# Two hybrid decoder layers on one core: the second block's values projected by token, its 64 sample tokens in narrow products of their own

## The chip, the cores and the metric

The kernel runs on one core of a Trainium2 chip. The metric is the time of one execution on the device, in microseconds, as the median of the runs shown.

## The reference

Two decoder layers over 1024 prompt tokens and 64 sample tokens (8 sequences of 8), width 1024, float32. Layer 0 mixes tokens with an mLSTM, layer 1 with gated linear attention (GLA); each is followed by a SwiGLU feed-forward network, and each part is wrapped in RMS norms. Cut to what the change touches:

```python
def mlstm_mixer(x, w_in, ...):
    proj = jnp.einsum('bsd,de->bse', x, w_in)
    q, k, v, o, ig, fg = jnp.split(proj, ...)      # 512, 512, 1024, 1024 columns, gates
    ...
    num = jnp.einsum('bhls,bshv->bhlv', A, vc) + ...     # values with tokens as rows
    C_new = ... + jnp.einsum('bshd,bshv->bhdv', kw, vc)
    y = jax.nn.sigmoid(o) * head_rms_norm(h, g_head)

def gla_mixer(x, w_in, ...):
    q, k, v, r, glr = jnp.split(proj, ...)
    o_intra = jnp.einsum('bhls,bshv->bhlv', A, vc)
    y = jax.nn.silu(r) * head_rms_norm(o, g_head)
```

So both mixers take a projected value matrix `v` of 1024 columns, and both multiply it with the token as the contracted index.

## The kernel before, in words

**Tokens and blocks.** The tokens lie in two blocks: block 0 holds 512 prompt tokens, block 1 holds the other 512 prompt tokens and the 64 sample tokens (576). Activations are kept with features on the 128 partitions and tokens in columns: `HH[b]` and `HL[b]`, a high and a low part of each number, of type fp32r. Weights come from HBM in tiles of 128 x 1024 (`w_stage`, three slots), and are split into `w_hi` (ScalarE, line 1444) and `w_lo` (VectorE, line 1796). A dense product is three matmuls for each of eight slices k of the contracted width: `w_lo` with HH, `w_hi` with HH, `w_hi` with HL.

**Units.** `Plan` writes the whole program out as a list of units of one weight tile each: P (mixer projections; 25 for each layer and block: unit 0 the gates, 1 to 8 q and k, 9 to 16 the values, 17 to 24 the output gate), W (output projection), G, U and D (feed-forward). A unit of block 0 is 24 matmuls of 512 columns; one of block 1 is 24 pairs of 288 columns into two PSUM banks (`GW`, line 1002). The small steps of the mixers and norms are tags on units: an engine runs its part of a tag behind its part of the unit. Every engine walks the same list in order. Banks 0 to 3 of PSUM are for units, banks 4 to 7 (`M0` = 4) for the mixers.

**Values of block 0** are projected token-major (`turned`, line 1007). The stationary operand is the activation of 128 tokens, and 512 columns of weights stream past it. Four units (`u.part` 0 to 3, each with two slices k) fill four banks, one for each chunk of 128 tokens; at part 3 the banks are evicted (line 1469 or 1818), and stored by token in `value_scratch` (`VD`). A mixer step loads its chunk from there (`values`, line 801) straight into its operand `V`.

**Values of block 1** are projected like all else, with features on partitions, and stored in `proj_scratch` (`PT`). For each chunk c of 4 to 8 (8 is the samples) the mixer loads them as `vt` (lines 798 and 866), turns them on TensorE with eight transposes (`v_turns`, line 1230) and copies them from PSUM to `V` on ScalarE (`v_copy`, line 1642). The semaphores `v_turned` and `v_copied` count these through `TURNS`.

**Where it stands.** Layer 0: block 1's units P 0 to 14, then the eight W of block 0, then P 15 to 24, then feed-forward units of block 0, on which the mixer steps of block 1 hang: `mload` loads at the first of them, `ma` (scores), `mb` (output), `md` (state), `me` (gating) follow. Block 0's own mixer steps hang on P units 22 to 24 of block 0 and 0 to 13 of block 1. Layer 1: P 0 to 24 of block 1, with `lload` on unit 21, then feed-forward units with `la`, `l1`, `l2`, `lb`, `le`. SyncE issues all loads and stores in the same order of units; evictions go through three slots of `evicted` (`E`), which a store must have left (semaphore `stored`) before they are written again.

```python
for m, (w, x) in enumerate(((wlo, hi), (whi, hi), (whi, lo))):
    for t in range(NG[blk]):
        mm = pe.matmul(ps[:, grp.bank + t, 0:W], wsl(w, k), x[:, k, t * W:(t + 1) * W], ...)
```

Of the kernel before, what the change touches and what calls it, by code (L numbers as in the profile page):

```python
# [13 lines left out]
P = 128  # L14
D = 1024
KD = D // P
# [31 lines left out]
NPROJ = 25  # L48
NW = 3
# [6 lines left out]
class Unit:  # L56
# [3 lines left out]
    def __init__(self, kind, layer, blk, i, j=0):  # L60
# [9 lines left out]
        self.part = (i - 9) % 4 if kind == "P" and blk == 0 and 9 <= i < 17 else None  # L70
# [24 lines left out]
class Plan:  # L95
# [50 lines left out]
    def banks(self):  # L146
# [3 lines left out]
        for u in self.units:  # L150
            by = "dve" if u.kind in "UD" or u.late else "act"
            if u.part is not None:
                if u.part == 0:
                    mine = [Group(0, (at + c) % 4, {held[(at + c) % 4][0]: held[(at + c) % 4][1]}, 0) for c in range(4)]
                if u.part < 3:
                    u.groups.append(Group(n, None, {}, 0))
                    n += 1
                for c, grp in enumerate(mine if u.part == 3 else ()):
                    counts[by] += 1
                    grp.n, grp.ev = n, counts[by]  # L160
                    held[grp.bank] = (by, grp.ev)
# [28 lines left out]
def schedule(plan):  # L190
# [62 lines left out]
    u = mlstm(plan, 0, [(u, u + 1, u + 3, u + 4) for u in range(at["P", 0, 0, 22, 0], at["P", 0, 1, 13, 0], 4)])  # L253
# [34 lines left out]
    u = gla(plan, 1, at["P", 1, 1, 21, 0], [at["G", 1, 0, i, 0] for i in (6, 8, 10, 12, 14)])  # L288
# [40 lines left out]
def mlstm(plan, blk, slots):  # L329
# [18 lines left out]
def gla(plan, blk, first, slots):  # L348
# [3 lines left out]
    for c, u in zip(CHUNKS[blk], slots):  # L352
# [6 lines left out]
        tag(u, "la", c)  # L359
        tag(u + 1, "l1" if c < NC else "l2", c)  # L360
# [80 lines left out]
def memory(nc, ctx):  # L441
# [96 lines left out]
    g.VD = nc.dram_tensor("value_scratch", [2, 4, P, H * DV], F32, kind="Internal").ap()  # L538
# [27 lines left out]
def program(nc, g, plan, a):  # L566
# [42 lines left out]
    def TURNS(layer, c):  # L609

        return 5 * layer + c - 3
# [34 lines left out]
    for u in units:  # L646
# [4 lines left out]
        if u.part is not None:  # L651
            u.places = []
            for c in range(4 if u.part == 3 else 0):
# [53 lines left out]
    with nc.Block() as block:  # L707
        @block.sync
        def _(sp):
# [43 lines left out]
            def evicted(u):  # L753
                if u.kind != "P" or u.i == 0:
                    return
                if u.part is not None:
                    for c, (slot, _) in enumerate(u.places):
                        sp.wait_ge(s["left_dve" if u.late else "left_act"], u.groups[c].ev)
                        sp.dma_start(g.VD[u.layer, c, :, (u.i - 12) * P:(u.i - 8) * P], g.E[:, slot, 0:NT[0]]
                                     ).then_inc(s["stored"][slot], 16)  # L760
# [27 lines left out]
            def m_qkv(c):  # L788
# [6 lines left out]
                if c < 4:  # L795
                    return
                wait(sp, s["v_turned"], TURNS(0, c) - 1)
# [3 lines left out]
            def values(layer, c):  # L801
# [3 lines left out]
                             ).then_inc(s["values_landed"], 16)  # L805

# [54 lines left out]
            def l_v(c):  # L861
                if c < 4:
                    values(1, c)
                    return
# [4 lines left out]
            def lload(c):  # L869
                blk = BLOCK(c)  # L870
                region_free(1, blk)
                landed(1, blk, 16)
                sp.wait_ge(s["b_stored"], 64 * (blk + 1))
                l_qkb(c)
                l_v(c)

            def l_o(c):
                if c in (0, 4):
                    landed(1, BLOCK(c), 24)
                if c >= 4:  # L880
                    sp.wait_ge(s["v_turned"], TURNS(1, c))
# [23 lines left out]
            def me(c):  # L905
                if c < 3:
# [24 lines left out]
            def ss(layer, j):  # L931
                if j == 0 and layer:
                    sp.wait_ge(s["level_done"], 8 * NC + 4)
                elif j == 0:
                    sp.wait_ge(s["s_ready"], NC + 1)
                    sp.wait_ge(s["k_turned"], NC + 1)
                    sp.wait_ge(s["v_turned"], TURNS(0, NC))
# [1530 lines left out]
```

## Time and profile before

| | |
|---|---|
| median of 3 runs | 2584.54 us (2583.43 to 2585.45) |
| profiled execution | 2585.84 us, span 2584.1 us |
| TensorE (PE) | 2567.6 us busy, 99% of the span, 17163 instructions |
| VectorE (DVE) | 1499.2 us, 58% |
| ScalarE (ACT) | 1011.8 us, 39% |
| DMA, hardware queue | 327.79 MB, 40.7% of 16 engines' span |
| chain that ended last | PE 93%, DVE 5%, ACT 2%, issue 1% |

A row of matmuls gives the sum or the mean of their durations, and one matmul's duration covers its way through a pipeline in which the next has begun. What one costs in a stream is therefore read from starts, not from durations: from the start of one row of the timeline to that of a later one, divided by the matmuls between. One matmul of float32 operands leaves two records, one of fp32r operands and one transpose leave one. PEld is the load of the stationary operand that belongs to each matmul.

### The profile page before, as it was taken

To read this page: it belongs to the slowest core of one execution; us is meant where nothing else is said; L and a number is where in the kernel's file an instruction comes from. 1 tells how busy PE (TensorE), PEld (TensorE's weight loads), DVE (VectorE), ACT (ScalarE), POOL (GpSimd) and SP (SyncE) were. 2 spreads that over 40 slices of the span, in tenths; PEclk is the share of its full clock that TensorE was granted. 3 is DMA by queue.
4 is the path that set the end of the run, shared out by engine and by line. 5 is a ranking of instruction groups with operands and counts; after the bars stand their busy time and mean duration, and the time that the engine had idled before them with its cause. 6 is when DMAs were issued, how large, how long until landed. Compare 5 with 4: busy or idle time off the path is not lost.

```text
span 2584.1 us, 40632 instructions
## 1 busy us (share of the span) xinstructions
PE 2567.6 (99%) x17163; PEld 2322.6 (90%) x17163; DVE 1499.2 (58%) x2314; ACT 1011.8 (39%) x1452; POOL 0.2 (0%) x4
## 2 busy tenths in 40 slices
PE   9999999999999999999999999999999999999998
PEld 7899898887988998889999988998887989999998
DVE  6744575556466673357754776338776486434435
ACT  5343355452334342445424444335552343222222
POOL 0000000000000000000000000000000000000000
PEclk9999999999999999999999999999999999999999
DMA  6454545444433333553333343444346334322222
GB/s 222 136 176 155 142 154 161 139 119 154 149 118 106 127 103 98 170 160 95 111 104 105 95 154 110 141 151 125 111 133 189 119 111 141 103 83 83 87 83 91
DMA packets 176704, 330.38 MB, mean 128 GB/s; under 512 B 19964, under 2 KB 93436, under 8 KB 176524
## 3 DMA queue, kind: packets, MB, share of 16 engines
q1 hardware_dynamic: 176524, 327.79, 40.7%
q8 instruction: 136, 2.23, 0.4%
q14 instruction: 44, 0.36, 0.0%
HBM read 271.46 MB, written 56.28 MB: 127 GB/s over the span
## 4 chain that ended last, share of the span: by engine, by line
PE 93%; DVE 5%; ACT 2%; issue 1%; DMA 0%; SPq 0%; DVEq 0%; ACTq 0%
PE ps L1002 81%; PE ps L1016 3%; PE ps L1321 1%; PE ps L1029 1%; PE ps L1409 1%; PE ps L1400 1%; PE ps L1263 1%; DVE Y L1867 1%; PE ps L1251 1%; PE ps L1245 1%; PE ps L1127 1%; DVE w_lo L1796 0%; PE ps L1244 0%; PE ps L1354 0%; PE ps L1355 0%
## 5 line engine op out<-in xcount | busy, mean ns | idle before, releaser
L1002 PE MATMUL ps<-HH,w_lo 128*128 128x288 f32 (+1 forms) x3480 | 944.4, 328 | 0.2 <-DVE w_lo L1796 0.2
L1002 PE MATMUL ps<-HL,w_hi 128*128 128x288 f32 (+1 forms) x3480 | 933.7, 325 | 0.0
L1002 PE MATMUL ps<-HH,w_hi 128*128 128x288 f32 (+1 forms) x3480 | 933.4, 325 | 0.0
L1002 PEld LDWEIGHTS ps<-HH,w_lo 128*128 128x128 f32 x3480 | 589.9, 188 | 49.7 <-issue 5.8
L1796 DVE TENSOR_TENSOR w_lo<-w_stage,w_hi 128x1024 fp32r<-128x1024 f32 x392 | 478.6, 1221 | 258.2 <-ACT w_hi L1444 257.0
L1002 PEld LDWEIGHTS ps<-HL,w_hi 128*128 128x128 f32 x3480 | 589.0, 188 | 42.8
L1002 PEld LDWEIGHTS ps<-HH,w_hi 128*128 128x128 f32 x3480 | 589.1, 188 | 40.8
L1444 ACT ACTIVATE w_hi<-w_stage 128x1024 fp32r<-128x1024 f32 x392 | 412.1, 1052 | 342.5 <-PE ps L1002 307.8
L1867 DVE TENSOR_TENSOR Y<-ps,Y 128x512 f32<-128x512 f32 (+1 forms) x319 | 226.5, 720 | 148.7 <-PE ps L1002 147.8
L1002 PE MATMUL ps<-hid_hi,w_lo 128*128 128x288 f32 (+1 forms) x1052 | 291.4, 331 | 3.1 <-DVE Y L1867 2.5
L1002 PE MATMUL ps<-hid_hi,w_hi 128*128 128x288 f32 (+1 forms) x1052 | 286.9, 327 | 0.0
L1002 PE MATMUL ps<-hid_lo,w_hi 128*128 128x288 f32 (+1 forms) x1052 | 286.8, 327 | 0.0
L1515 ACT ACTIVATE hid_hi<-evicted 128x512 fp32r<-128x512 f32 (+1 forms) x88 | 57.9, 658 | 363.8 <-DVE evicted L1849 363.8
L1002 PEld LDWEIGHTS ps<-hid_hi,w_lo 128*128 128x128 f32 x1052 | 178.4, 188 | 23.1 <-DVE Y L1867 5.9
L1002 PEld LDWEIGHTS ps<-hid_lo,w_hi 128*128 128x128 f32 x1052 | 178.8, 188 | 13.9
L1002 PEld LDWEIGHTS ps<-hid_hi,w_hi 128*128 128x128 f32 x1052 | 178.8, 188 | 13.1
L1849 DVE TENSOR_TENSOR evicted<-ps,evicted 128x512 f32<-128x512 f32 (+1 forms) x88 | 63.5, 722 | 145.5 <-PE ps L1002 145.4
L1807 DVE TENSOR_TENSOR n_sum<-n_sum,n_sq 128x512 f32<-128x512 f32 (+1 forms) x110 | 79.4, 722 | 93.0 <-ACT n_sq L1450 89.1
L1511 ACT ACTIVATE evicted<-ps 128x512 f32<-128x512 f32 (+1 forms) x88 | 54.8, 623 | 176.8 <-PE ps L1002 176.4
L1484 ACT ACTIVATE evicted<-ps 128x576 f32<-128x576 f32 (+1 forms) x64 | 40.8, 637 | 211.3 <-PE ps L1002 211.1
L1852 DVE TENSOR_TENSOR hid_lo<-evicted,hid_hi 128x512 fp32r<-128x512 f32 (+1 forms) x88 | 63.8, 725 | 63.8 <-ACT hid_hi L1515 63.8
L1450 ACT ACTIVATE n_sq<-n_xs 128x512 f32<-128x512 f32 (+1 forms) x64 | 41.6, 657 | 91.2 <-DVE n_xs L1909 84.4
(260 smaller groups left out, 1891.3 us busy)
## 6 DMA issues: line engine op xcount, KB each, us to landing
w_stage<-w_gate_in SPq DMA_DIRECT2D x88, 512.0 KB, 3.6
w_stage<-w_up_in SPq DMA_DIRECT2D x88, 512.0 KB, 3.7
w_stage<-w_down_in SPq DMA_DIRECT2D x88, 512.0 KB, 3.6
w_stage<-w_in_in SPq DMA_DIRECT2D x80, 512.0 KB, 3.8
w_stage<-w_out_in SPq DMA_DIRECT2D x32, 512.0 KB, 3.8
proj_scratch<-evicted SPq DMA_DIRECT2D x48, 288.0 KB, 2.2
proj_scratch<-evicted SPq DMA_DIRECT2D x32, 256.0 KB, 2.1
w_stage<-w_v_in SPq DMA_DIRECT2D x16, 512.0 KB, 4.1
```

What stands on the lines that cost most here:

```text
L1002: mm = pe.matmul(ps[:, grp.bank + t, 0:W], wsl(w, k), x[:, k, t * W:(t + 1) * W], start=(k == first and m == 0), stop=(k == last and m == 2))
L1016: mm = pe.matmul(ps[:, grp.bank, :], x[:, k, t], w[:, n % NW, cols], start=(k == 0 and m == 0), stop=(k == KD - 1 and m == 2))
L1444: act.activation(g.whi[:, n % NW, :], g.wst[:, n % NW, :], ACT.Copy).then_inc(s["w_hi"], 1)
L1450: act.activation(grouped(dst, b) if src.shape != dst.shape else dst, src, ACT.Square).then_inc(s["squared"], 1)
L1484: act.activation(grouped(g.E[:, u.slot, 0:NT[b]], b), bank(grp.bank, b), func, scale=scale).then_inc(s["left_act"], 1)
L1511: act.activation(grouped(g.E[:, c, 0:NT[b]], b), bank(grp.bank, b), ACT.Silu).then_inc(s["left_act"], 1)
L1515: act.activation(g.hh[:, u.i % 2, 0:NT[b]], g.E[:, 2, 0:NT[b]], ACT.Copy).then_inc(s["hid_hi_ready"], 1)
L1796: dve.tensor_tensor(g.wlo[:, n % NW, :], g.wst[:, n % NW, :], g.whi[:, n % NW, :].bitcast(F32), ALU.subtract).then_inc(s["w_lo"], 1)
L1807: dve.tensor_tensor(acc, acc, sq, ALU.add).then_inc(s["summed"], 1)
L1849: dve.tensor_tensor(grouped(pr, b), bank(grp.bank, b), grouped(g.E[:, u.i % 2, 0:NT[b]], b), ALU.mult).then_inc(s["left_dve"], 1)
L1852: dve.tensor_tensor(g.hl[:, u.i % 2, 0:NT[b]], pr, g.hh[:, u.i % 2, 0:NT[b]].bitcast(F32), ALU.subtract).then_inc(s["hid_lo_ready"], 1)
L1867: dve.tensor_tensor(Y, bank(grp.bank, b), Y, ALU.add).then_inc(s["left_dve"], 1)
```

## The change

Three things change, in both layers:

- The projections of block 1 are made in another order (`PROJ`): units 0 to 8, then 17 to 24 (output gate), then 9 to 16 (values). Positions of all tags stay where they were by number, so that with the first 15 positions of layer 0 now stand output gates where values stood.
- The values of block 1's 512 prompt tokens are projected as those of block 0 are: token-major, four units into four banks, 5 evictions at part 3, and stored in `value_scratch`, which now has room for all eight chunks. Chunks 4 to 7 are loaded from there, and their transposes and copies are gone. Only the samples (chunk 8) keep `vt`, eight transposes and a copy.
- The values of the 64 sample tokens are projected in `sample_values`, called as a fifth chunk of each value unit: for each of four output tiles of 128 features, two slices k and three matmuls, of 64 columns each, into bank 6, which is one of the mixers'. Before the first of them PE waits for the mixer steps that used the bank, and the first mixer step behind them (`ma(4)`, `la(4)`) waits for its eviction.

The functions `mload` and `lload` no longer wait for the values; a new step `vload` does, on the unit of `ma(4)` or `la(4)`.

```diff
+PROJ = (tuple(range(NPROJ)), tuple(range(9)) + tuple(range(17, 25)) + tuple(range(9, 17)))
+SAMPLE_BANK = 6
...
-        self.part = (i - 9) % 4 if kind == "P" and blk == 0 and 9 <= i < 17 else None
+        self.part = (i - 9) % 4 if kind == "P" and 9 <= i < 17 else None
...
-        for i in range(i0, i1):
+        for i in PROJ[blk][i0:i1]:
             self.put(Unit("P", layer, blk, i))
...
                     mine = [Group(0, (at + c) % 4, {held[(at + c) % 4][0]: held[(at + c) % 4][1]}, 0) for c in range(4)]
+                    if u.blk:
+                        mine.append(Group(0, SAMPLE_BANK, {}, 0))
...
-        if blk:
-            tag(a + blk, "mv", c)
+        if c == 4:
+            tag(a, "vload", c)
...
-    def TURNS(layer, c):
-
-        return 5 * layer + c - 3
+    def TURNS(layer):
+
+        return layer + 1
...
+                        if c < 4:
+                            sp.dma_start(g.VD[u.layer, 4 * u.blk + c, :, (u.i - 12) * P:(u.i - 8) * P], g.E[:, slot, 0:NT[0]]
+                                         ).then_inc(s["stored"][slot], 16)
+                        else:
+                            sp.dma_start(g.PT[u.i - 4:u.i, :, span(NC)].rearrange("q p t -> p q t"),
+                                         g.E[:, slot, 0:4 * TS].rearrange("p (q t) -> p q t", q=4)
+                                         ).then_inc(s["stored"][slot], 16)
...
+            def vload(c):
+                layer = 0 if vloads.pop() else 1
+                landed(layer, 1, 16)
+                values(layer, c)
...
-                landed(0, blk, 16)
+                landed(0, blk, 8 if blk else 16)
...
+            def sample_values(n, u, grp):
+
+
+                HH, HL = g.HH[1], g.HL[1]
+                if u.part == 0 and u.layer == 0:
+                    pe.wait_ge(s["nat_copied"], 2)
+                    pe.wait_ge(s["gate_act"], 10)
+                    pe.wait_ge(s["state_added"], 4)
+                elif u.part == 0:
+                    pe.wait_ge(s["z_abs"], 8)
+                if u.part == 0 and u.i > 9:
+                    pe.wait_ge(s["left_act"], unit("P", u.layer, 1, 12).groups[4].ev)
+                for q in range(4):
+                    for j in range(2):
+                        k, cols = 2 * u.part + j, slice(j * 512 + q * P, j * 512 + (q + 1) * P)
+                        for m, (x, w) in enumerate(((HH, g.wlo), (HH, g.whi), (HL, g.whi))):
+                            mm = pe.matmul(ps[:, grp.bank, q * TS:(q + 1) * TS], w[:, n % NW, cols], x[:, k, 512:576],
+                                           start=(q == 0 and k == 0 and m == 0),
+                                           stop=(q == 3 and k == KD - 1 and m == 2))
+                return mm
...
             def turned(n, u):
 
+                HH, HL = g.HH[u.blk], g.HL[u.blk]
                 for c, grp in enumerate(u.chunks):
                     if u.part == 0:
                         free(grp)
+                    if c == 4:
+                        mm = sample_values(n, u, grp)
                     t = slice(c * L, (c + 1) * L)
-                    for j in range(2):
+                    for j in range(2 if c < 4 else 0):
...
             def ma(c):
                 n = SIZE(c)
+                if c == 4:
+                    pe.wait_ge(s["left_act"], unit("P", 0, 1, 16).groups[4].ev)
...
-                if c >= 4:
+                if c == NC:
                     v_turns(c, 1, g.x.VT)
```

**TensorE, a value unit of block 1.** Before, each of the 16 such units (8 in each layer) is 24 of these rows (`HH`, `HL` the activations, `w_lo`, `w_hi` the weights, `ps` PSUM):

```order
L1002 MATMUL ps<-HH,w_lo 128x288 x2
L1002 MATMUL ps<-HH,w_hi 128x288 x2
L1002 MATMUL ps<-HL,w_hi 128x288 x2
L1002 MATMUL ps<-HH,w_lo 128x288 x2
L1002 MATMUL ps<-HH,w_hi 128x288 x2
L1002 MATMUL ps<-HL,w_hi 128x288 x2
```

Now the unit ends its fourth chunk of prompt tokens, and the samples' products follow it:

```order
L1060 MATMUL ps<-w_lo,HH 128x512
L1060 MATMUL ps<-w_hi,HH 128x512
L1060 MATMUL ps<-w_hi,HL 128x512
L1043 MATMUL ps<-HH,w_lo 128x64
L1043 MATMUL ps<-HH,w_hi 128x64
L1043 MATMUL ps<-HL,w_hi 128x64
L1043 MATMUL ps<-HH,w_lo 128x64
L1043 MATMUL ps<-HH,w_hi 128x64
L1043 MATMUL ps<-HL,w_hi 128x64
```

In place of 24 pairs of 288 columns a unit has 24 matmuls of 512 columns and 24 of 64; in all units there are 384 of the narrow ones.

**TensorE, the step `la` of layer 1 for a chunk of prompt tokens** (`l_vt` the loaded values, `l_k_decayed` the keys, both turned with the identity `ident`). Before:

```order
L1002 MATMUL ps<-HH,w_lo 128x512
L1002 MATMUL ps<-HH,w_hi 128x512
L1002 MATMUL ps<-HL,w_hi 128x512
L1230 MATMUL ps<-ident,l_vt 128x128 x8
L1303 MATMUL ps<-ident,l_k_decayed 128x128 x4
```

Such eight transposes stand at eight places before (four chunks in each layer), and at none now; those of the samples stay at two.

**ScalarE, the steps of block 0's chunk 3 in layer 0**, beside block 1's projections (`evicted` the evictions, `m_scores` the decays of `ma`, `m_y_normed` the squares of `mb`). Before:

```order
L1484 ACTIVATE evicted<-ps 128x576
L1669 ACTIVATE HH<-m_y_gated 128x8x128
L1625 ACTIVATE m_scores<-m_scores,per_token 128x128 x4
L1630 ACTIVATE m_k_weighted<-ps,per_token 128x128 x4
L1444 ACTIVATE w_hi<-w_stage 128x1024
L1484 ACTIVATE evicted<-ps 128x576
L1651 ACTIVATE m_y_normed,small<-ps,small 128x256 x4
```

Now:

```order
L1533 ACT_TABLE_LOAD
L1533 ACTIVATE evicted<-ps 128x576
L1718 ACTIVATE HH<-m_y_gated 128x8x128
L1481 ACT_TABLE_LOAD
L1674 ACTIVATE m_scores<-m_scores,per_token 128x128 x4
L1679 ACTIVATE m_k_weighted<-ps,per_token 128x128 x4
L1492 ACTIVATE w_hi<-w_stage 128x1024
L1533 ACT_TABLE_LOAD
L1533 ACTIVATE evicted<-ps 128x576
L1481 ACT_TABLE_LOAD
L1700 ACTIVATE m_y_normed,small<-ps,small 128x256 x4
```

Four loads of function tables have come in, since the evictions there are now sigmoids of the output gate. In the whole program ScalarE has 112 of them where it had 105.

## Rows read from the trace of the kernel before

**Rows 1.** The page: busy time, granted clock and the chain that ended last.

```profile
PE 2567.6 (99%) x17163; PEld 2322.6 (90%) x17163; DVE 1499.2 (58%) x2314; ACT 1011.8 (39%) x1452; POOL 0.2 (0%) x4
...
PEclk9999999999999999999999999999999999999999
...
PE 93%; DVE 5%; ACT 2%; issue 1%; DMA 0%; SPq 0%; DVEq 0%; ACTq 0%
```

**Rows 2.** Waits of PE, longest in total.

```profile
PE ps L1029 <- DVE HL L2343: 2.8, 2, 2.2
PE ps L1002 <- DVE Y L1867: 2.5, 6, 0.7
```

**Rows 3.** PE timeline (start, duration), block 1's units: 42 pairs lie between.

```profile
341.18 0.43 PE L1002 MATMUL ps<-HH,w_hi 128*128 128x288 f32 x2
...
352.38 0.43 PE L1002 MATMUL ps<-HH,w_hi 128*128 128x288 f32 x2
```

**Rows 4.** PE timeline, block 0's value units in layer 0: first and last of 192.

```profile
61.03 0.40 PE L1016 MATMUL ps<-w_lo,HH 128*128 128x512 f32 x1
...
104.72 0.39 PE L1016 MATMUL ps<-w_hi,HL 128*128 128x512 f32 x1
```

**Rows 5.** PE timeline at the transposes of chunk 4, layer 0.

```profile
398.68 0.39 PE L1002 MATMUL ps<-HH,w_hi 128*128 128x512 f32 x1
398.90 0.39 PE L1002 MATMUL ps<-HL,w_hi 128*128 128x512 f32 x1
399.13 1.04 PE L1230 MATMUL ps<-ident,m_vt 128*128 128x128 f32 x8
399.92 0.48 PE L1002 MATMUL ps<-HH,w_lo 128*128 128x512 f32 x1
400.24 0.39 PE L1002 MATMUL ps<-HH,w_hi 128*128 128x512 f32 x1
```

**Rows 6.** Line L1384: durations in ns min/median/max, first and last start in us.

```profile
L1384 PEld LDWEIGHTS ps<-batch_rows,m_k_weighted x8: 183/188/188, 648.4 to 649.2; 64*128 64x128 f32 x8
L1384 PE MATMUL ps<-batch_rows,m_k_weighted x8: 252/252/273, 648.4 to 649.2; 64*128 64x8 f32 x8
```

**Rows 7.** Timeline of PE and PEld at narrow matmuls of one column and of 128.

```profile
43.07 0.96 PEld L1186 LDWEIGHTS ps<-ones,Y 1*128 1x128 f32 x8 [0.35 <-issue]
...
138.91 1.05 PE L1215 MATMUL ps<-m_qk 128*128 128x128 f32 x8
...
139.80 0.60 PE L1219 MATMUL ps<-ident,m_qk 128*128 128x128 f32 x4
```

**Rows 8.** Weight loads by shape: count, busy us, mean ns.

```profile
L1002 PEld LDWEIGHTS ps<-HL,w_hi 128*128 128x128 f32 x3480 | 589.0, 188 | 42.8
...
L1263 PEld LDWEIGHTS ps<-ident,m_y_normed 128*128 128x128 f32 x64 | 7.5, 140 | 0.5
```

**Rows 9.** ScalarE timeline at block 0's chunk 3, layer 0.

```profile
231.48 0.65 ACT L1484 ACTIVATE evicted<-ps 128x576 f32<-128x576 f32 x1 [6.53 <-PE ps L1002]
233.61 1.06 ACT L1669 ACTIVATE HH<-m_y_gated 128x1024 fp32r<-128x1024 f32 x1 [1.48 <-DVE m_y_gated L2109]
236.63 1.28 ACT L1625 ACTIVATE m_scores<-m_scores,per_token 128x128 f32<-128x128 f32 x4 [1.96 <-DVE m_scores L2051]
...
240.08 0.65 ACT L1484 ACTIVATE evicted<-ps 128x576 f32<-128x576 f32 x1 [0.21 <-PE ps L1002]
244.35 0.47 ACT L1651 ACTIVATE m_y_normed<-ps,small 128x256 f32<-128x256 f32 x1 [3.62 <-DVE small L2068]
```

**Rows 10.** Line L1484: durations in ns of its table loads.

```profile
L1484 ACT ACT_TABLE_LOAD  x8: 1283/1283/1283, 332.8 to 1746.1; - x8
```

**Rows 11.** Line L1469, block 0's value evictions in layer 1, and their idle time.

```profile
L1469 ACT ACTIVATE evicted<-ps x8: 598/598/599, 1062.6 to 1088.4; 128x512 f32<-128x512 f32 x8
...
DMA value_scratch<-evicted: 2.6, 1
```

**Rows 12.** DMA issues: count, KB each, median us to landing.

```profile
value_scratch<-evicted SPq DMA_DIRECT2D x16, 256.0 KB, 2.3
...
m_v_one<-value_scratch SPq DMA_DIRECT2D x4, 512.0 KB, 4.5
```

**Rows 13.** Windows of 2 us: busy us of PE, PEld, DVE, ACT, POOL, then granted clock.

```profile
1760.00:1762.00 2.00, 2.00 (x86) 1.76 (x85) 2.00 (x7) 0.66 (x1) 0.00 (x0) 1.00 0.09 35
...
1766.00:1768.00 2.00, 2.00 (x133) 1.57 (x131) 1.90 (x4) 1.06 (x1) 0.00 (x0) 1.00 0.59 119
```

More of the change, by code:

```diff
@@ L160, in banks @@
                     grp.n, grp.ev = n, counts[by]
-                    held[grp.bank] = (by, grp.ev)
+                    if c < 4:
+                        held[grp.bank] = (by, grp.ev)
                     u.groups.append(grp)
@@ L252, in schedule @@
         tag(at["P", 0, 0, 12, 0] + 2 * j, t, 0, j)
-    u = mlstm(plan, 0, [(u, u + 1, u + 3, u + 4) for u in range(at["P", 0, 0, 22, 0], at["P", 0, 1, 13, 0], 4)])
+    u = mlstm(plan, 0, [(u, u + 1, u + 3, u + 4) for u in range(at["P", 0, 0, 22, 0], at["P", 0, 1, 0, 0] + 13, 4)])
     assert u <= at["W", 0, 0, 0, 0], (u, at["W", 0, 0, 0, 0])
@@ L359, in gla @@
         tag(u, "la", c)
+        if c == 4:
+            tag(u, "vload", c)
         tag(u + 1, "l1" if c < NC else "l2", c)
@@ L652, in program @@
             u.places = []
-            for c in range(4 if u.part == 3 else 0):
+            for c in range(4 + u.blk if u.part == 3 else 0):
                 u.places.append((turn % 3, stores[turn % 3]))
@@ L861, in l_v @@
             def l_v(c):
-                if c < 4:
+                if c < NC:
                     values(1, c)
@@ L905, in me @@
             def me(c):
-                if c < 3:
+                if c < NC - 1 and c != 3:
                     values(0, c + 1)
@@ L954, in sh @@
                     sp.dma_start(a["n_out"], g.NS[:, :]).then_inc(s["outs"], 16)
-            steps = {"xpart": xpart, "xload": xload, "xstore": xstore, "mload": mload, "mb": mb, "md": md, "lg": lgate, "lload": lload,
+            steps = {"vload": vload, "xpart": xpart, "xload": xload, "xstore": xstore, "mload": mload, "mb": mb, "md": md, "lg": lgate, "lload": lload,
                      "lvt": l_v, "l1": l_o, "lb": lb, "me": me, "la": la, "le": le, "l2": l2, "ss": ss, "sh": sh, "mg3": rows, "last": last}
@@ L1226, in v_turns @@
                 n = SIZE(c)
-                pe.wait_ge(s["vt_landed"], 16 * TURNS(layer, c))
+                pe.wait_ge(s["vt_landed"], 16 * TURNS(layer))
                 wait(pe, s["y_gated"], 9 * layer + c)
@@ L1294, in la @@
                 n = SIZE(c)
+                if c == 4:
+                    pe.wait_ge(s["left_act"], unit("P", 1, 1, 16).groups[4].ev)
                 if c in (0, 4):
@@ L1468, in evict @@
                             wait(act, s["hid_lo_ready"], u.hid0)
-                            act.activation(g.E[:, slot, 0:NT[0]], ps[:, grp.bank, :], ACT.Copy).then_inc(s["left_act"], 1)
+                            cols = slice(0, 4 * TS if grp.bank == SAMPLE_BANK else NT[0])
+                            act.activation(g.E[:, slot, cols], ps[:, grp.bank, cols], ACT.Copy).then_inc(s["left_act"], 1)
                         return
@@ L1637, in v_copy @@
                 n = SIZE(c)
-                if c < 4:
+                if c < NC:
                     return
-                act.wait_ge(s["v_turned"], TURNS(layer, c))
+                act.wait_ge(s["v_turned"], TURNS(layer))
                 wait(act, s["kv"], NC * layer + c)
@@ L1666, in y_high @@
                 if c in (0, 4):
-                    act.wait_ge(s["groups"], unit("P", layer, b, 24).groups[0].n + 1)
+                    act.wait_ge(s["groups"], unit("P", layer, b, PROJ[b][-1]).groups[-1].n + 1)
                 act.wait_ge(s["y_gated"], 9 * layer + c + 1)
@@ L2273, in prepare @@
                     wait(dve, s["k_copied"], 9 * layer + NC + 1)
-                    wait(dve, s["v_turned"], TURNS(layer, NC))
+                    wait(dve, s["v_turned"], TURNS(layer))
                     dve.memset(x.QB[:, :, :], 0.0).then_inc(s["qb_zeroed"], 1)
```

39 lines of the change are left out of this document (20 added, 19 removed).

## Prediction, made before the changed kernel was run

> **What bounds the kernel now.** I read the page first: TensorE (PE) is busy 99% of the span, it makes up 93% of the chain that ended last, and its clock is granted in full in every slice [rows 1]. Then the waits of PE: the longest entry in total is 2.8 us and the next 2.5 us, out of 2584 [rows 2]. So no wait is there to be won; the time is the sum of what stands on PE's queue, and whatever changes that sum by 1 us changes the time by about 1 us. Busy time does not price a matmul, since the durations overlap. I therefore take every price from starts in the timeline.
>
> **The change, part by part.**
>
> *Prompt values.* A value unit of block 1 is 24 pairs of 288 columns. From 341.18 to 352.38 us lie 42 pairs: 11.20 / 42 = 0.2667 us a pair, 133 ns a matmul, and 24 x 0.2667 = 6.40 us a unit [rows 3]. The prompt part of the new unit is what block 0 has already: 191 intervals from 61.03 to 104.72 us, 43.69 / 191 = 0.2287 us each, waits and evictions of the four banks included, so 24 x 0.2287 = 5.49 us [rows 4]. Each of the 16 units gives back 0.91 us: **-14.6 us**.
>
> *Transposes.* Around chunk 4's eight transposes the second dense matmul before them starts at 398.90 and the second after them at 400.24, 1.34 us where two plain steps of 227 ns would take 0.455 [rows 5]. Eight transposes cost 0.88 us. They go at eight places: **-7.1 us**. The eight copies to `V` on ScalarE go too; that engine is 39% busy and they were hidden, so nothing.
>
> *Sample values.* 16 units x 24 = 384 matmuls of 64 columns are added, and their price p decides. The trace has no fp32r matmul below 288 columns. Bounds: from above, the 133 ns of the 288 columns, which have the same type and the same load of weights [rows 3]. From below, columns alone: 512 columns take 227 ns [rows 5] and 288 take 133, so 0.42 ns a column, and 64 columns would take 39 ns. Between the ends the nearest rows are those of narrow matmuls with a full load of 128 weight columns. At L1384 (8 columns) eight start between 648.4 and 649.2, about 110 ns apart [rows 6]. With one column eight loads span 0.96 us, of which the last is 0.19, so 7 steps in 0.77, 110 ns; with 128 columns eight start in 139.80 - 138.91 = 0.89 us, 111 ns each [rows 7]. Whether 1, 8 or 128 columns stream, the step is the same: the load sets it. These are float32, but their load lasts 188 ns as the fp32r one does (188), while a load that is quicker shows 140 [rows 6, 8]. So p is at least 111. What fp32r adds: 288 columns at 2.4 GHz are 120 ns and cost 133, 512 are 213 and cost 227 [rows 3, 5], about 10 ns more over the bare columns than float32's 111 has over the same load. If that gap stays when the load binds, p is 121. I take the middle, **116 ns**: 384 x 0.116 = **+44.5 us**; the ends 111 and 133 give 42.6 and 51.1.
>
> The Trainium skill speaks of this price twice in "TensorE: Matmul & The Clock Gate". Its section "LDWEIGHTS (loading the stationary operand)" puts a load at P / 1.2 ns, 107 ns for 128 columns, which the 110 to 111 ns of rows 6 and 7 bear out. Its section "Back-to-back issue gap" puts a stream of loads and matmuls at about 81 ns for N = 128, and an isolated matmul at N / 2.4 + 2.5, an estimate of 29 ns here; by 81 ns the sum would be +9.4 us and by 29 ns -10.5 us, and against both stands the 111 ns of rows 7.
>
> *Order.* With the output gates moved ahead, ScalarE evicts sigmoids beside chunk 3's exponentials. A table load is 1.28 us [rows 10]. The four come at idle places: 6.53 us idle before the eviction at 231.48, 1.96 us before the exponentials at 236.63, and behind the eviction at 240.08 there are 3.62 us before the squares at 244.35, room for two loads (2.6 us) with 1.0 to spare [rows 9]. The other three of the seven added stand beside W units and the norm, with a unit's idle time of 5 to 6 us around each. Cost 0; if that cover were gone, the output step would be up to 2.6 us late, and PE needs it only two units (12.8 us) later.
>
> *Evictions and stores.* At part 3 five evictions are made where four units made one each. They last 0.60 us [rows 11] and the groups end 6 x 0.229 = 1.37 us apart, the samples' last. A slot of `evicted` comes round after three, 4.1 us, and needs 0.60 + 2.3 for eviction and landing [rows 11, 12]. No wait in the mean. Block 0's quad in layer 1 shows one such wait of 2.6 us on ScalarE, and none of PE behind it [rows 2, 11]. SyncE's queue has five stores in a row at part 3, but has issued the next weights ahead of them. `vload` makes SyncE wait for the last value stores, one unit after they were issued, with the next weights already under way; chunk 4's values then need 4.5 us [rows 12] and are wanted two units (11 us) later. PE's new waits for bank 6 are for steps that are units old (`state_added` of chunk 3, the gate steps), or for an eviction that has the next unit's 5.5 us of prompt products to finish. Each 0.
>
> *Sum:* -14.6 - 7.1 + 44.5 = **+22.8 us**. The profiled execution took 2585.84 us, so its like would take 2608.6; the median of the runs is 1.3 us lower, and I forecast 2584.54 + 22.8 = **2607.3 us**. A difference under 0.2%, 5.2 us, can't be told from none here.
>
> **The rivals.**
>
> 1. *The load of weights hides, and the columns alone are paid* (faster). p = 39 ns gives 384 x 0.039 = 15.0, and the sum is 15.0 - 21.7 = -6.7 us: 2577.8. It decides below p = 21.7 / 384 = 56 ns. For it: the loads are seen to start while the matmul before is still running. Against it: rows 6 and 7, where nothing but the load can take 110 ns for one column. The skill's isolated gap above is this case. Chance 0.06.
> 2. *A load faster than float32's, not hidden,* p between 60 and 95 ns, say 81: +9.4 us, 2593.9. Only if fp32r loads differ inside equal durations of 188 ns [rows 8]. The skill's figure for N = 128 is this case. Chance 0.06, of which a third falls within 0.2%.
> 3. *Load and stream don't overlap fully,* p = 133 or a little more: +29.4 us, 2613.9. For it: it is what the widths nearest to it cost in fp32r. Against: 128 float32 columns, whose stream is as long as their load, show 111 and no addition [rows 7]. Chance 0.12.
> 4. *A new wait:* evictions into three slots hold the banks, and PE stands at the first chunk of the second quad, or at `ma(4)`. If each of the four quads cost 2.6 us, the one slot wait that the trace shows [rows 11], it is 10.4 us more: 2617.7. Chance 0.06.
> 5. *The clock falls* during narrow products, since little of the array's work is done in them. The windows with 86 and 133 small matmuls in 2 us keep 1.00 [rows 13], and a run of narrow ones lasts here 24 x 0.116 = 2.8 us between 5.5 us of dense work. Were the prompt part then at half the clock, 16 x 5.49 = 88 us would come on top. Chance 0.02.
>
> My forecast, p from 105 to 127 ns with no wait over 2 us, has the remaining 0.68.
>
> **How the numbers follow.** The forecast's own range is 384 x 0.105 - 21.7 = +18.6 to 384 x 0.127 - 21.7 + 2 = +29.1, 2603 to 2614. To hold 8 in 10 with the bounds' width I take in rival 3 whole and part of rival 4 above, and some way towards rival 2 below: 2598 to 2617. Left out are rivals 1, 2, 5 and half of 4, 0.17. Faster by over 0.2%: rival 1, 0.06. Within 0.2%: a third of rival 2, 0.02, and 0.01 for p around 60. Slower: the rest, 0.91.
>
> **What would show it.** In the changed profile: starts of the narrow matmuls (L1043) 111 to 121 ns apart, a value unit 8.2 to 8.4 us long in place of 6.40; starts of L1060's matmuls in block 1 0.229 us apart as in block 0; no transposes between 399 and 500 us except the samples'; PE's waits for ScalarE and bank 6 near 0; the granted clock full. Wrong would be: a step of the narrow ones well outside 105 to 133 ns (the load's price is not what rows 6 and 7 show), or PE waits of more than 2 us in value units or at the first mixer step behind them.

## The result, and the profile after

The changed kernel takes **2605.96 us** (median of 4 runs, 2605.4 to 2606.64) against 2584.14 us before in the same comparison (4 runs, 2583.43 to 2585.45): ratio 1.0084, 95% interval 1.0071 to 1.0097. It is 21.8 us slower; forecast were +22.8 us and 2607.3 us.

The page of the changed kernel, the same parts as [rows 1]:

```profile
span 2603.9 us, 40493 instructions
...
PE 2588.8 (99%) x17099; PEld 2327.8 (89%) x17099; DVE 1498.9 (58%) x2314; ACT 1015.9 (39%) x1455; POOL 0.2 (0%) x4
...
PEclk9999999999999999999999999999999999999999
...
PE 92%; DVE 5%; ACT 2%; issue 1%; DMA 0%; SPq 0%; DVEq 0%; ACTq 0%
```

TensorE still fills the span, at a full clock. Note that it has 64 instructions fewer than before and 21 us more busy time: the count says nothing here.

Waits of PE in the changed kernel, the two longest (engine, line, releaser: us in total, times, longest):

```profile
PE ps L1022 <- DVE Y L1916: 2.5, 6, 0.7
PE ps L1466 <- DVE state L2385: 1.4, 1, 1.4
```

In the whole list nothing waits for bank 6, for an eviction of values or for ScalarE. So the new time is on PE's queue itself.

Timeline of PE in the changed kernel, the end of the first value unit of layer 0 and the start of the second (start, duration, both us):

```profile
332.81 0.39 PE L1060 MATMUL ps<-w_hi,HL 128*128 128x512 f32 x1
333.03 0.19 PE L1043 MATMUL ps<-HH,w_lo 128*128 128x64 f32 x1
333.06 0.28 PE L1043 MATMUL ps<-HH,w_hi 128*128 128x64 f32 x1
333.17 0.28 PE L1043 MATMUL ps<-HL,w_hi 128*128 128x64 f32 x1
...
335.52 0.28 PE L1043 MATMUL ps<-HL,w_hi 128*128 128x64 f32 x1
335.63 0.48 PE L1060 MATMUL ps<-w_lo,HH 128*128 128x512 f32 x1
335.95 0.40 PE L1060 MATMUL ps<-w_hi,HH 128*128 128x512 f32 x1
...
343.78 0.48 PE L1060 MATMUL ps<-w_lo,HH 128*128 128x512 f32 x1
```

Three things are to be read from it:

- From 333.06 to 335.52 lie 22 steps: 2.46 / 22 = **0.112 us** for a product of 64 columns. This is the step of float32's one and 128 columns in [rows 7].
- At the edges of the block a load can be seen to hide under the matmul ahead of it. The first narrow product, behind a wide one, is done with after 0.03 us (0.19 us of duration, where the others have 0.28 and wait for their load in it). The first wide one, behind a narrow one, keeps the engine 0.32 us instead of 0.227 (0.48 us of duration, not 0.39). The sum is that of 24 full steps: 0.03 + 23 x 0.112 + 0.09 = 2.7 us, and 24 x 0.112 = 2.68.
- The second unit runs from 335.63 to 343.78, 8.15 us, where the forecast had 8.2 to 8.4 and the old unit took 6.40 [rows 3].

The loads of these products, by line (ns min/median/max), last 192 ns, about as long as the others' 188 [rows 8]:

```profile
L1043 PEld LDWEIGHTS ps<-HL,w_hi x128: 191/192/192, 333.1 to 1770.3; 128*128 128x128 f32 x128
```

**Where the 21.8 us are, by place.** The same instruction is looked up in both traces at five places where the order is the same in both. Timeline of PE, before (the norm ahead of the value units; the outputs of chunks 4 and 7 in layer 0; the gate step and the first level step of chunk 4 in layer 1):

```profile
322.87 0.40 PE L1146 MATMUL ps<-n_sum_parts,avg_r 128*128 128x512 f32 x1
405.48 0.60 PE L1244 MATMUL ps<-state,m_q_weighted 128*128 128x257 f32 x2
529.25 0.60 PE L1244 MATMUL ps<-state,m_q_weighted 128*128 128x257 f32 x2
1652.22 0.75 PE L1288 MATMUL ps<-Y,w_gate 32*128 32x288 f32 x4
1759.44 0.33 PE L1321 MATMUL ps<-l_levels 128*64 128x64 f32 x2
```

And of the changed kernel:

```profile
320.72 0.62 PE L1190 MATMUL ps<-n_sum_parts,avg_r 128*128 128x512 f32 x2
416.37 0.60 PE L1290 MATMUL ps<-state,m_q_weighted 128*128 128x257 f32 x2
537.47 0.60 PE L1290 MATMUL ps<-state,m_q_weighted 128*128 128x257 f32 x2
1660.40 1.00 PE L1334 MATMUL ps<-Y,w_gate 32*128 32x288 f32 x6
1781.99 0.39 PE L1369 MATMUL ps<-l_levels 128*64 128x64 f32 x3
```

The difference after minus before is -2.15, +10.89, +8.22, +8.18, +22.55 and, at the end of the spans, +19.8 us. Layer 0's value units and the first set of transposes gone make +13.04; three more sets make -2.67, 0.89 each. Over the 1100 us between, nothing moves (-0.04). Layer 1's units and its first set make +14.37, the three other sets -2.75. From the norm on, the sum is +22.0 us.

The -2.15 us at the front is no work of the change. It is the first 30 us, where the two profiled executions differ in clock (columns: window, its length, busy us and instructions of PE, PEld, DVE, ACT, POOL, granted clock, DMA share, GB/s). Before:

```profile
0.00:30.00 30.00, 25.72 (x93) 20.18 (x94) 18.89 (x26) 19.98 (x28) 0.20 (x4) 0.89 0.59 193
```

and the changed kernel:

```profile
0.00:30.00 30.00, 27.07 (x103) 19.95 (x104) 20.94 (x29) 20.00 (x28) 0.20 (x4) 1.00 0.58 193
```

In the trace of before the first dense products ran at the lower level (a granted clock of 0.55 from 10 to 15 us against 1.00; 0.63 us of duration against 0.40 to 0.50), and waits for `HL` of 2.8 us [rows 2] became one of 1.3. The change does not touch this stretch. This is why the two profiled spans lie only 19.8 us apart, while the places where the change acts add up to 22.0 and the medians differ by 21.8.

### The profile page after: what moved, and what is told of

It reads as the page before. It is cut to its first block, busy times and chain, and to the rows that moved or that the text cites. A ratio compares the mean times of both kernels' runs of the same rounds, so it can differ in the third digit from the quotient of the medians.

```text
span 2603.9 us, 40493 instructions
## 1 busy us (share of the span) xinstructions
PE 2588.8 (99%) x17099; PEld 2327.8 (89%) x17099; DVE 1498.9 (58%) x2314; ACT 1015.9 (39%) x1455; POOL 0.2 (0%) x4
## 4 chain that ended last, share of the span: by engine, by line
PE 92%; DVE 5%; ACT 2%; issue 1%; DMA 0%; SPq 0%; DVEq 0%; ACTq 0%
PE ps L1022 76%; PE ps L1060 6%; PE ps L1043 2%; DVE Y L1916 1%; PE ps L1369 1%; PE ps L1457 1%; PE ps L1448 1%; PE ps L1309 1%; PE ps L1297 1%; PE ps L1291 1%; DVE w_lo L1845 1%; PE ps L1171 0%; ACT w_hi L1492 0%; PE ps L1073 0%; PE ps L1290 0%
## 5 line engine op out<-in xcount | busy, mean ns | idle before, releaser
L1022 PE MATMUL ps<-HH,w_lo 128*128 128x288 f32 (+1 forms) x3224 | 889.7, 330 | 0.1
L1022 PE MATMUL ps<-HL,w_hi 128*128 128x288 f32 (+1 forms) x3224 | 879.3, 327 | 0.0
L1022 PE MATMUL ps<-HH,w_hi 128*128 128x288 f32 (+1 forms) x3224 | 879.2, 327 | 0.0
L1022 PEld LDWEIGHTS ps<-HH,w_lo 128*128 128x128 f32 x3224 | 548.8, 188 | 49.7 <-issue 5.8
L1022 PEld LDWEIGHTS ps<-HL,w_hi 128*128 128x128 f32 x3224 | 547.9, 188 | 42.9
L1022 PEld LDWEIGHTS ps<-HH,w_hi 128*128 128x128 f32 x3224 | 547.9, 188 | 40.8
L1060 PE MATMUL ps<-w_lo,HH 128*128 128x512 f32 x256 | 101.0, 394 | 0.1
L1060 PE MATMUL ps<-w_hi,HH 128*128 128x512 f32 x256 | 99.8, 390 | 0.0
```

The lines of the kernel that those rows point to most:

```text
L1060: mm = pe.matmul(ps[:, grp.bank, :], x[:, k, t], w[:, n % NW, cols], start=(k == 0 and m == 0), stop=(k == KD - 1 and m == 2))
```

## The experiments

Eight kernels were run. The narrow products stand at line 1043, as in the changed kernel, or near it where lines have gone; all diffs but the last are against the changed kernel, and are cut to the products. The kernel before was timed anew beside each group of runs, with medians of 2584.0 to 2584.8 us, so a difference between kernels of two groups is uncertain by some 0.8 us.

### Twice the columns (e1_w128)

The narrow products stream 128 columns:

```diff
-    mm = pe.matmul(ps[:, grp.bank, q * TS:(q + 1) * TS], w[:, n % NW, cols], x[:, k, 512:576], ...)
+    mm = pe.matmul(ps[:, grp.bank, q * P:(q + 1) * P], w[:, n % NW, cols], x[:, k, 448:576], ...)
```

> The 384 narrow products stream 128 columns instead of 64 (64 prompt tokens go in with the 64 of the samples, so the sample values come out as other numbers); everything else is the changed kernel, 2606.0 us. Load theory: a narrow product costs its load of 128 weight columns, 111.6 ns in the trace, and 128 columns at 2.4 GHz are 53 ns and hide in it. Steps stay at 112 ns and the time at 2606, within 2 us. Rival, price by columns in a slow mode: 64 columns at four cycles each are 107 ns and would look the same in the changed kernel; 128 columns would then be 213 ns or more, a step of about 217, so 384 x 0.105 = +40 us, 2646.

Measured: 2607.29 us (2606.97 to 2607.51), ratio 1.0087 (1.007 to 1.0104): 1.3 us over the changed kernel. Timeline of PE in this run:

```profile
334.21 0.28 PE L1043 MATMUL ps<-HH,w_hi 128*128 128x128 f32 x1
...
336.56 0.27 PE L1043 MATMUL ps<-HH,w_hi 128*128 128x128 f32 x1
```

21 steps in 2.35 us, 0.112 each, as with 64 columns. Only the first product of each block, whose load is hidden, is dearer: it is followed after 0.058 us instead of 0.03, 16 x 0.03 = 0.5 us in all. The rest of the 1.3 us is within what two groups differ by. So where the load is not hidden, twice the columns cost nothing: the columns are not what is paid.

### The narrow products left out (e2_none)

```diff
-    for q in range(4):
-        for j in range(2):
...
+    return pe.matmul(ps[:, grp.bank, 0:4 * TS], g.whi[:, n % NW, 0:P], HH[:, 2 * u.part, 320:576],
+                     start=u.part == 0, stop=u.part == 3)
```

> The 24 narrow products of each value unit are left out, and one of 256 columns stands in their place so that the bank is written (the sample values are not computed). If the narrow products cost what the starts in the trace say, 2.69 us a unit, the time falls by 16 x 2.69 = 43.0 less 16 x 0.12 = 1.9, to 2565, 19 us below the kernel before: 14.6 + 7.1 less 1.9, or a little more. Rival, part of the 22 us sits in waits or in the new order: then it falls by clearly less than 41 us or stays away from 2565 by more than 3.

Measured: 2569.56 us (2568.87 to 2569.78), ratio 0.9941 (0.9926 to 0.9956). That is 36.4 us under the changed kernel, and 4.6 us above the 2565 that were expected, outside the 3 us that the expectation allowed. In layer 1 the eight value units and what is left of the fifth chunk lie between 1689.76 and 1734.4 us, 44.64 us, which is 8 x 5.46 for the wide products and 8 x 0.12 for the one product. In layer 0 they take 48.06 us, 3.4 more, of which 0.5 are the norm's matmul that stands among them in both kernels. The other 3 us are in the main idle time of PE, and its waits have entries which the changed kernel does not have (`issue`: the profile names nothing that PE waited for); behind them the timeline of PE, where the two parts of the first entry stand:

```profile
PE ps L1022 <- issue: 2.7, 2, 1.6
...
PE ps L1054 <- ACT evicted L1512: 0.9, 1, 0.9
...
376.21 0.47 PE L1022 MATMUL ps<-HH,w_lo 128*128 128x512 f32 x1 [1.61 <-issue]
...
1148.29 0.29 PE L1022 MATMUL ps<-HH,w_hi 128*128 128x288 f32 x1 [1.07 <-issue]
```

The 0.9 us are a wait for ScalarE's evictions, at 351.5 us. At 376.21, behind the last value unit of layer 0, ScalarE and VectorE had been busy beside these units with a norm of block 0, and ScalarE came to split the next weights only at 374.58 and to empty the banks at 375.53. So 5.6 us of work in a unit no longer cover what the two have to do there; for the 1.6 us this is read from the place, and no run tests it. The 1.07 us at 1148 stand in the middle of a unit, 770 us behind, and from there on this kernel is 1.3 us later than the changed one; the cause is open.

The sum of prices, 384 x 0.112 - 16 x 0.113 = 41.2 us, is right for PE's own instructions and wrong for the kernel. The two profiled spans lie 36.1 us apart. Of the 5.1 us between, 3.0 are cover that layer 0 lost, 1.3 appear at 1148 us, and 0.6 are a difference in the first 30 us, which the edit does not touch. So the mark of the expectation's rival was reached, but not its content, that part of the 22 us sits in waits or in the new order: the waits came in with this edit, and the changed kernel has none of them.

### The narrow products spread out (e3_inter)

One narrow product behind each wide one (`sample_values` is a generator from which `turned` draws one after each matmul):

```diff
+                            last = mm
+                            if u.blk:
+                                narrow = next(samples)
```

> The same products, but each narrow one follows a wide one of 512 columns. In the changed kernel the first narrow product behind a wide one takes only 29 ns and the wide one behind the last takes 317. Load theory: each load starts only when the matmul ahead of it starts, so a wide and a narrow one take 227 + 112 in any order: 2606, within 3 us, with steps of about 30 and 310. Rival, the loads could be spread under the wide products (more than one load ahead): a narrow one costs its columns and a gap, 40 ns, so 384 x 0.072 = 28 us less, 2578.

Measured: 2608.95 us, ratio 1.0094 (1.0079 to 1.0109), 3.0 us over the changed kernel. Timeline of PE in this run:

```profile
332.97 0.48 PE L1060 MATMUL ps<-w_hi,HH 128*128 128x512 f32 x1
333.29 0.19 PE L1043 MATMUL ps<-HH,w_hi 128*128 128x64 f32 x1
333.32 0.47 PE L1060 MATMUL ps<-w_hi,HL 128*128 128x512 f32 x1
333.62 0.19 PE L1043 MATMUL ps<-HL,w_hi 128*128 128x64 f32 x1
333.65 0.48 PE L1060 MATMUL ps<-w_lo,HH 128*128 128x512 f32 x1
```

A wide and a narrow product together take 0.34 us (332.97, 333.32, 333.65), the same 0.227 + 0.112 as in a block. Only the place of the cost moves: each narrow product starts 0.30 to 0.32 us behind a wide one and is followed after 0.03. The rows of the loads in the same stretch show why:

```profile
333.05 0.19 PEld L1043 LDWEIGHTS ps<-HH,w_hi 128*128 128x128 f32 x1
333.29 0.19 PEld L1060 LDWEIGHTS ps<-w_hi,HL 128*128 128x128 f32 x1
```

The narrow product's load begins at 333.05, under the wide product of 332.97, which has room for it. The next wide product's load does not follow it there; it begins at 333.29, when the narrow one starts, and finds 0.03 us of cover. So a load hides under the one matmul ahead of it. Mixing narrow and wide products buys nothing. Of the 3 us more, 1.4 are PE's waits for an eviction at the start of each layer's second quad, and some 3 ns a pair are 1.2 (95 pairs from 1707.14 to 1739.65 us, 0.342 each, against 0.339).

### Half the weight columns (e5_w64) and a quarter (e9_w32)

If the load is paid, the number of weight columns is the price, whatever is streamed. The diff is that of e5_w64; e9_w32 has 32 in place of 64. The products' output and its eviction have as many rows as there are weight columns:

```diff
-    k, cols = 2 * u.part + j, slice(j * 512 + q * P, j * 512 + (q + 1) * P)
+    k, cols = 2 * u.part + j, slice(j * 512 + q * P, j * 512 + q * P + 64)
```

> The changed kernel, but each of the 384 narrow products takes only the first 64 of its 128 weight columns (half of the sample values are not computed); it streams 64 columns as before. Load theory: the step follows the width of the load; the kernel before has 64 weight columns with 64 streamed at L1215 for the samples, eight starts in 0.61 us, 76 ns. So 384 x (0.1116 - 0.076) = 13.7 us less than 2606.0: 2592. Rival, a fixed cost of about 110 ns for any narrow fp32r product, or one for its streamed columns: nothing moves, 2606.

> As e5_w64, but the narrow products take only 32 of each quarter's 128 weight columns, so three quarters of the samples' values are not computed. Steps measured so far are 111.7 ns with 128 weight columns and 58.4 with 64: 0.833 ns a weight column and 5.1 ns beside. Load theory: 32 weight columns give 32 x 0.833 + 5.1 = 31.8 ns a step, a run of 24 lasts 0.75 us, and the kernel is 368 x 0.080 = 29.4 us under the changed one, about 2576.6. Rival, the stream of 64 columns binds first: the columns' price of 39 ns a step, which the wide points give, 368 x 0.0727 = 26.8 us under, 2579.2. Rival, a fixed cost of an instruction near 58 ns, which would have made e5_w64's step: 58 ns, 2586.

Measured: e5_w64 2586.55 us (2585.68 to 2587.87), ratio 1.0008 (0.9999 to 1.0017); e9_w32 2576.85 us (2576.15 to 2577.05), ratio 0.9972 (0.9959 to 0.9984), against 2576.6 expected. Timeline of PE, e5_w64:

```profile
333.26 0.22 PE L1043 MATMUL ps<-HH,w_hi 128*64 128x64 f32 x1
...
334.54 0.22 PE L1043 MATMUL ps<-HL,w_hi 128*64 128x64 f32 x1
```

and e9_w32:

```profile
333.29 0.20 PE L1043 MATMUL ps<-HH,w_hi 128*32 128x64 f32 x1
...
333.99 0.20 PE L1043 MATMUL ps<-HL,w_hi 128*32 128x64 f32 x1
```

22 steps in 1.28 us are 0.058 each with 64 weight columns; 22 in 0.70 are 0.032 with 32. With 128 it is 0.112. The step falls with the weight columns at 0.83 ns each, over some 5 ns that stay. The first of the two fell by more than expected (19.4 us instead of 13.7), since the expectation had put the step at 76 ns. That was a misreading of the trace of before: it divided the stretch of eight float32 products by eight, and the first and the last of them are followed only after 0.11 and 0.15 us. Timeline of PE, before, twice the same row cut at different places:

```profile
557.43 0.51 PE L1215 MATMUL ps<-m_qk 128*64 128x64 f32 x6
...
557.72 0.22 PE L1215 MATMUL ps<-m_qk 128*64 128x64 f32 x1
```

Five steps in 0.29 us are 0.058 each, the price that e5_w64 then showed in fp32r: with 64 weight columns, too, the two types cost the same. The second was foretold from 112 and 58 and came within 0.3 us. At 32 the stream of 64 columns (27 ns at 2.4 GHz) is about as long as the load, and the single steps there scatter; where one limit hands over to the other is not told apart.

The Trainium skill, "TensorE: Matmul & The Clock Gate", section "LDWEIGHTS (loading the stationary operand)", has a load at P / 1.2 ns, by estimate 107, 53 and 27 ns for these three; the traces' slope is that one, with about 5 ns a step on top. The figure of 81 ns for N = 128 in its section "Back-to-back issue gap" is not borne out by any run here: e1_w128 has 112.

### Where the stream takes over (e7_c256)

The narrow products stream 256 columns, all into the first half of the bank:

```diff
-    mm = pe.matmul(ps[:, grp.bank, q * TS:(q + 1) * TS], w[:, n % NW, cols], x[:, k, 512:576], ...)
+    mm = pe.matmul(ps[:, grp.bank, 0:256], w[:, n % NW, cols], x[:, k, 320:576], ...)
```

> The 384 narrow products stream 256 columns (320 to 576) instead of 64, all into the first 256 columns of their bank, so the samples' values are not computed. The question is where the price of a load ends and that of a stream begins. Load-or-stream theory: the step is the larger of the load's 112 ns, as with 64 and 128 columns, and the stream's, which by the two wide points (288 columns 133 ns, 512 columns 227 ns, 0.42 ns a column) is 120 ns at 256; so steps of 120 ns and 368 x 0.008 = 3 us more than the changed kernel, about 2609. Rival, a load that covers a stream of its own length without the stream's own gap: steps stay at 112 ns, 2606. Rival, load and stream add up in part: steps of 133 ns or more, 2614 or more.

Measured: 2609.27 us (2 runs, 2608.58 to 2609.96), ratio 1.0098 (1.0069 to 1.0127). Timeline of PE:

```profile
332.78 0.28 PE L1043 MATMUL ps<-HH,w_hi 128*128 128x256 f32 x1
...
335.42 0.28 PE L1043 MATMUL ps<-HL,w_hi 128*128 128x256 f32 x1
```

22 steps in 2.64 us, 0.120 each, as foretold. So 64 and 128 columns cost 112 ns, 256 cost 120, 288 cost 133 and 512 cost 227. On the straight line through the last three, 0.42 ns a column, 112 ns is reached at about 237 columns: below that a product with 128 weight columns costs its load.

### The samples' values by token too (e4_tok)

If the load of 128 weight columns is what is paid, the small operand should be the stationary one. The 64 sample tokens become the stationary operand and 512 weight columns stream past: 6 products a unit in place of 24. The samples' values come out with tokens as rows, so their transposes and copies go as well, and chunk 8 is loaded from `value_scratch` like the others.

```diff
-                for q in range(4):
-                    for j in range(2):
-                        k, cols = 2 * u.part + j, slice(j * 512 + q * P, j * 512 + (q + 1) * P)
-                        for m, (x, w) in enumerate(((HH, g.wlo), (HH, g.whi), (HL, g.whi))):
-                            mm = pe.matmul(ps[:, grp.bank, q * TS:(q + 1) * TS], w[:, n % NW, cols], x[:, k, 512:576], ...)
+                for j in range(2):
+                    k, cols = 2 * u.part + j, slice(j * 512, (j + 1) * 512)
+                    for m, (x, w) in enumerate(((HH, g.wlo), (HH, g.whi), (HL, g.whi))):
+                        mm = pe.matmul(ps[0:TS, grp.bank, :], x[:, k, 512:576], w[:, n % NW, cols], ...)
```

> The samples' values are also projected token-major: the stationary operand is the activation of the 64 sample tokens, and 512 columns of weights stream past it, 6 matmuls a unit in place of 24; stored by token and loaded like the rest, so that the samples' eight transposes and the copy in each layer go too. Load theory: a wide matmul costs its columns, 0.2287 us, whatever its stationary operand is wide: 6 x 0.2287 = 1.37 us a unit in place of 2.69, 16 x 1.32 = 21.1 less, and about 0.9 in each layer for the transposes: 2606.0 - 22.9 = 2583, as the kernel before. Rival, the loss lies in the fifth group itself (its bank, its waits, five evictions into three slots): then little of the 22 us comes back and the time stays above 2595.

Measured: 2584.07 us (10 runs, 2583.68 to 2584.59), ratio 0.9998 (0.9988 to 1.0007): what the change had lost is back, no more. Timeline of PE in this run, the start of layer 1's first value unit, and of the unit behind its last:

```profile
1695.07 0.39 PE L1046 MATMUL ps<-w_lo,HH 128*128 128x512 f32 x1
...
1749.65 0.39 PE L1010 MATMUL ps<-HH,w_lo 128*128 128x512 f32 x1
```

A value unit takes 54.58 / 8 = 6.82 us, which is 30 x 0.2274. Against the old 6.40 and 6.25 that is 0.42 and 0.57 us too many in each of 2 x 8 units, 7.9 us, and the eight sets of transposes gone give 7.1 back, the samples' two a little more.

### High and low part side by side (e6_stack)

Two of the six products have the same streamed operand, `w_hi`, and stationary operands of 64 columns each (HH and HL of the samples). VectorE puts these side by side (`sample_hi_lo`, 128 columns), one product then makes both, in the lower and the upper 64 partitions, and the halves are added at the eviction. The diff is against e4_tok:

```diff
-                    for m, (x, w) in enumerate(((HH, g.wlo), (HH, g.whi), (HL, g.whi))):
-                        mm = pe.matmul(ps[0:TS, grp.bank, :], x[:, k, 512:576], w[:, n % NW, cols], ...)
+                    both = ((slice(0, P), g.S[u.layer][k // 4][:, k % 4, :], g.whi), (slice(0, TS), HH[:, k, 512:576], g.wlo))
+                    for m, (rows, x, w) in enumerate(both if k == 0 else both[::-1]):
+                        mm = pe.matmul(ps[rows, grp.bank, :], x, w[:, n % NW, cols], ...)
...
+                    dve.tensor_tensor(g.E[0:TS, slot, 0:NT[0]], ps[0:TS, grp.bank, :], g.E[0:TS, slot, 0:NT[0]], ALU.add
+                                      ).then_inc(s["halves"], 1)
```

> As e4_tok, but the high and low part of the 64 sample tokens stand side by side in one stationary operand of 128 columns (copied there once a layer by VectorE, into rows of Y that are free), so that one matmul streams w_hi past both and a second one w_lo past the high part: 4 matmuls of 512 columns a unit in place of 6. The two halves are added at the eviction, ScalarE copying one and VectorE adding the other. If a wide matmul costs its streamed columns whatever stands, 16 x 2 x 0.2287 = 7.3 us less than e4_tok's 2584.1: 2576.8, 7 to 8 us below the kernel before. Rival, the eviction in two steps and the copies on VectorE put waits where e4_tok had none: 2579 to 2584.

Measured: **2576.14 us** (6 runs, 2575.24 to 2576.57), ratio 0.9967 (0.9955 to 0.998). Timeline of PE, the end of the first value unit:

```profile
333.09 0.39 PE L1057 MATMUL ps<-w_hi,HL 128*128 128x512 f32 x1
333.32 0.39 PE L1041 MATMUL ps<-w_hi,sample_hi_lo 128*128 128x512 f32 x1
333.54 0.63 PE L1041 MATMUL ps<-w_lo,HH 128*64 128x512 f32 x2
334.01 0.39 PE L1041 MATMUL ps<-w_hi,sample_hi_lo 128*128 128x512 f32 x1
334.23 0.39 PE L1057 MATMUL ps<-w_lo,HH 128*128 128x512 f32 x1
```

Four products, 0.91 us from 333.32 to 334.23, where the narrow ones took 2.68. VectorE's part is hidden: PE has no wait for `sample_hi_lo` or the added halves. This kernel is 8.5 us under the kernel before, timed beside it, and 29.8 under the changed kernel, the fastest here that leaves nothing out.

## Why the prediction was right, and by how much each step

**What bounds the kernel.** Right: all of the difference is on PE's queue, and no engine or queue shows a new wait on it.

**Prompt values, -14.6 us.** Right in kind, 0.8 us too large. The new prompt part takes 24 x 0.2274 = 5.46 us instead of 5.49 (the 192 steps of [rows 4] included small waits). But the old unit had two prices. In layer 1 the pairs of 288 columns ran faster than in [rows 3]; timeline of PE, before:

```profile
1661.30 0.42 PE L1002 MATMUL ps<-HH,w_lo 128*128 128x288 f32 x2
...
1670.66 0.42 PE L1002 MATMUL ps<-HH,w_lo 128*128 128x288 f32 x2
```

36 pairs in 9.36 us, 0.260 each, so 6.25 us a unit (the 15 projection units up to 1747 us take 93.71). The saving was 8 x 0.94 + 8 x 0.79 = 13.8 us. The price had been read in one place and used in two.

**Transposes, -7.1 us.** Right: the differences fall by 0.89 us at each set in layer 0, and six of the eight sets alone make 2.67 + 2.75 = 5.4. (The row of 398.90 that the prediction calls the second dense matmul before them is the last one; the stretch of 1.34 us and its price are right.)

**Sample values, +44.5 us.** Right in mechanism, 1.5 us too large. Measured were 384 x 0.112 = 43.0 us. What failed is the half-way allowance of 116 ns for what fp32r might add to float32's 111: it adds nothing while the load binds. The 13 ns by which 288 columns exceed their bare 120 belong to the stream; e1_w128 and e7_c256 show that they appear only once the stream is the longer of the two. The lower end, the row of the nearest operation with the same load [rows 7], was the price. One of the reasons given for that row carried nothing: that these loads last 188 ns like fp32r's while quicker ones show 140. The transposes' loads last 140 ns in the trace of before, and eight of them still took 0.88 us [rows 5], 110 ns each. How long a load's row lasts does not by itself tell its price.

**Order, evictions, stores, new waits, 0.** Right for PE, which loses nothing to them (between 537 and 1652 us the difference moves by 0.04). Seven table loads more and the fifth eviction are on ScalarE, which has the idle time. ScalarE's waits for a slot are 4.4 us in two instead of 2.6 in one [rows 11]; both stand at block 0's value evictions (1076.7 and 1097.7 us) and none at the new ones of block 1, and they did not reach PE. e2_none shows that the cover of the value units is not wide in layer 0: with 2.6 us less work in a unit, PE waits.

**Sum.** -13.8 - 7.1 + 43.0 = +22.1 us by the measured prices, +22.0 from the norm on in the traces, +21.8 in the medians; forecast +22.8. Two errors, 0.8 and 1.5 us, of opposite sign: that the sum came within 1 us is in part luck.

**The rivals.** That the load hides (2577.8) is refuted by the 0.112 us, by e1_w128 and e3_inter; a hidden load does occur, once in each block of 24, and costs 0.03 us there. A faster load of 81 ns and a serial step of 133 are refuted by the same rows. No new wait, and no fall of the clock: 1.00 in this window of the changed kernel, with a whole block of narrow products in it:

```profile
330.00:340.00 10.00, 10.00 (x58) 8.73 (x57) 8.93 (x13) 4.43 (x6) 0.00 (x0) 1.00 0.68 235
```

## What to carry to other kernels

In a stream of matmuls that each bring a stationary operand of their own, one costs the longer of two things, the load of that operand (here 0.83 ns a weight column and 5 ns, 112 ns for 128) and its stream (in fp32r 0.42 ns a column and 13 ns, from 256 columns on); so a narrow product with a full-width load is priced by the load, whether it stands in a block or between wide ones. Where few tokens meet a wide weight matrix, make the tokens the stationary operand and stream the weights; if they fill only 64 of the 128 weight columns, put two operands that meet the same stream side by side. Before taking work off the bounding engine, look at what it hides: in e2_none 3 of 20.6 us in layer 0 did not come back.

## What was not expected of the hardware

- In both kernels the pairs of 288 columns take 0.260 us from the gate step of layer 1 (1653 us before) to the last projection unit, and 0.265 to 0.267 us in nearly all of the rest, at a granted clock of 1.00 in both stretches. They are the same instructions on the same shapes. No run was made on it, and the cause is open; it is worth 1.2 us of this sum.
- A product of 64 columns behind a wide one is followed after 0.03 us. The line through the wide prices gives 0.039, so the 13 ns that a wide fp32r product has over its bare columns are not seen at 64 columns, nor at 128 (0.058 us in e1_w128, 53 ns of bare columns). A forecast of rival 1 by that line would have been too dear.
- Leaving work out of PE's queue made PE wait in layer 0's shorter units (e2_none), in a kernel where PE's waits were below 3 us for each releaser and TensorE was busy 99% of the span. In layer 1 the same units showed no wait.
- Loads whose rows last 140 and 188 ns [rows 6, 8] go at the same step of 110 ns (the transposes and the float32 products of before).
